# Value blending behind the chain, two tiles in turn, finer first transfers and new fillings in a hybrid decoder trunk

## The chip, the core and the metric

The kernel runs on one core of a Trainium2 chip. Its engines work side by side and meet only at semaphores: TensorE (PE) multiplies matrices, VectorE (DVE) and ScalarE (ACT) work elementwise, GpSimd (POOL) adds weights and issues transfers, SyncE (SP) issues transfers. SBUF is the memory that the engines read, PSUM the one that TensorE writes. The metric is the device time of one execution in microseconds; the table below gives it.

## The reference

One step of a trunk of two layers, for a prompt of 256 tokens and 8 sample tokens (264 columns) that share all weights. All is float32. Per layer:

```python
h = x @ w_in                                   # columns: mixer A, mixer B, merge gates
# mixer A, RWKV-7: token shift, decay, then a scan over time per head
S = S*w + (S @ a) b^T + v k^T ;  y = S @ r     # GroupNorm + bonus, times silu(z_A)
# in layer 1 the values are blended with those of layer 0 first:
vg = sigmoid(v0 + (v @ v1) @ v2) ;  v = v + (v_first - v) * vg
# mixer B, native sparse attention: compressed, selected and window branch,
# each softmax with a relative bias, gated per head, times silu(z_B)
m = sigmoid(g_A) * (o_A @ w_up_a) + sigmoid(g_B) * (o_B @ w_up_b)
x = layer_norm(ALPHA * x + m @ w_out)
```

The sample tokens read 256 earlier keys and values from pages of a cache and from a cache of window rows, and carry a 64x64 state per head.

## The kernel before

**Tiles of weights.** Activations lie transposed: `XT` holds 16 row tiles of 128 features by 264 columns, `H` the projected ones. A projected tile is 16 products of 128x128 weights (`WT`, two slots) with one tile of `XT`. One such product is a *unit*; the trace shows a unit as two instructions of line 760.

**Three kinds of product.** 46 tiles of a layer (`TILES`) are projected unit by unit by `project`. The others are computed in pairs of tiles with seven block products in place of eight (`main_pair`, `gate_pair`, `up_pair`, `out_pair`); those need sums of weight blocks, which POOL makes (`s1` the addition, `s3` the subtraction) and DVE (`s2`, `s4`), and sums of tokens, which DVE makes.

**The order, written by hand.** Each engine runs its own program. A layer goes: two tiles (`start`), 20 main pairs, four head quads of mixer A, the sample state, GroupNorm, compression, attention of the prompt (eight units), attention of the sample, four gate pairs, eight up pairs, eight out pairs, LayerNorm. From the head quads on these stages are chains of small products on PE with DVE and ACT between them. `plan()` gives each place in a chain a number of units (`BEHIND` for the quads, `BEHIND_MIX` after), and `project(place)` works tiles off up to that count while the chain's other engines compute. These are the *fillings*. What is left of the 46 tiles is worked off before the head quads' end (`mixers`) and before the gate pairs (`gates`). ACT takes each finished tile out of PSUM (`take_out`) at the same places.

**A head quad** (four heads, lines 1442 to 1501 on ACT, 1796 to 1917 on DVE, 979 to 1107 on PE): PE's `low` products; ACT's tanh; DVE computes decay, in layer 1 the blended values (`vd`, `vg`, `vm`, lines 1830 to 1834), then `kb`, `kf`, `kp`, `rk` (line 1843). PE fills with `low` units and waits for `rk` at line 1003. DVE goes on to `kt` (line 1856), for which PE waits at line 1012, then to the bonus (line 1859) and to `g4` (line 1865), which waits for line 1012.

**The sample's attention.** POOL loads the keys; when a product (`sc0`, `sc1`) has read them, it loads values into the same memory: per sequence two pages and one block of window rows (line 696). Line 1310 waits for them.

**Gate pair 0.** SP loads its four blocks when the attention's last DVE operation (`zb`, line 2145) is done, POOL then makes `s1` (line 715), which needs blocks 2 and 3, and `s3` (line 717), which needs 0 and 2.

**LayerNorm's tail** (lines 2323 to 2347): DVE centres the last four tiles, then tiles 0 to 11 in three operations (line 2328), waits for ACT's square root, takes the reciprocal (line 2339), multiplies in five groups (line 2343), scales tiles 12 to 15 (line 2346); ACT scales tiles 0 to 11 (line 1666). PE's first tile of layer 1 waits for these one by one.

**The first transfers.** SP loads `XT` in four parts and each tile of `WT` in two halves of 512 KB, in the order x, half, x, x, half, x, second tile, main pair 0.

Of the kernel before, what the change touches and what calls it, by code (L numbers as in the profile page):

```python
# [15 lines left out]
KT = D // P  # L16
# [72 lines left out]
HEAD_AT, HVAR_AT = 28, 48  # L89
FIRST = {}  # L90
# [25 lines left out]
def plan():  # L116

    upto = {}
    for L in range(DEPTH):
# [57 lines left out]
def hybrid_trunk(nc, ins, outs):  # L177
# [4 lines left out]
    with ExitStack() as ctx:  # L182
# [158 lines left out]
        d_x = [sem(f"x_loaded{q}") for q in range(4)]  # L341
        d_att = [sem("att_loaded0"), sem("att_loaded1")]
        st_shift, st_kv, st_wkv, st_swkv, st_win, st_y = (sem(n) for n in (
            "shift_stored", "kv_stored", "wkv_stored", "sample_wkv_stored", "window_copied", "y_stored"))
        w_in_slot = [[sem(f"weights_in_slot{s}{h}") for h in "ab"] for s in range(2)]
        w_in_main = [sem(f"weights_in_main{b}") for b in range(4)]
# [6 lines left out]
        def steps(phase, rounds, **engines):  # L353
            for e, names in engines.items():
# [9 lines left out]
              v=lambda it: ("lw one gate cum " + ("vd vg vm " if it >= NQUAD else "") + "kb kf kp rk at rt bt kt bon g40 g41 x0 x1 x2 lm1 "  # L364
# [23 lines left out]
        steps("os", DEPTH * BOTH, v="s2 s4", p="s1 s3")  # L388
        steps("ot", DEPTH, v="t1a t3a t2a t4a t1b t3b t2b t4b t1c t3c t2c t4c t1d t3d t2d t4d")
        steps("ln", DEPTH, t="head hvar mu var", v=" ".join(f"sum{i}" for i in range(1, HEAD)) + " hm hc0 sum12 sum13 hc1 hc2 ycb0 ycb1 d e" + "".join(f" yca{q}" for q in range(3)) + " rs "  # L390
              + " ".join(f"yn{q}" for q in range(5)) + " affv", a="hq0 hq1 hq2 hv sq0 sq1 sqrt " + " ".join(f"aff{i}" for i in range(SPLIT)))
# [72 lines left out]
        def _(sp):  # L464
            def load_x(q):
                sp.dma_start(XT[:, 4 * q:4 * q + 4, :], x_t[:, 4 * q:4 * q + 4, :]).then_inc(d_x[q], 16)
# [30 lines left out]
            def load_pairs(L):  # L497

                sp.wait_ge(*step("zb_v", L, "out"))
                for b in range(4):  # L500
                    load_block(L, 0, b)
# [42 lines left out]
            for n in range(DEPTH * N_TILES):  # L544
# [25 lines left out]
                for half in range(2):  # L570
                    sp.dma_start(WT[:, s, 8 * half:8 * half + 8, :], w_all[L, i, :, 8 * half:8 * half + 8, :]).then_inc(w_in_slot[s][half], 16)
                    if n == 0 and half == 0:
                        load_x(1)
                        load_x(2)
                    if n == 0 and half == 1:
                        load_x(3)
                    if n == 1 and half == 1:
                        for b in range(4):
                            load_main(L, 0, b)
            load_pairs(DEPTH - 1)  # L580
            for i, j in stores:
                if j <= SPLIT:
                    sp.wait_ge(*step("ln_a", DEPTH - 1, f"aff{j - 1}"))
                else:
                    sp.wait_ge(*step("ln_v", DEPTH - 1, "affv"))
# [4 lines left out]
        def _(po):  # L590
# [38 lines left out]
            for L in range(DEPTH):  # L629
# [69 lines left out]
                for g in range(BOTH):  # L699
# [3 lines left out]
                    if g:  # L703
                        po.wait_ge(*pair_step(L, g - 1, "st2"))
                        po.wait_ge(*step("os_v", L * BOTH + g - 1, "s2"))
# [20 lines left out]
        def _(pe):  # L726
# [6 lines left out]
            def project(*place):  # L733

                while at[0] < UPTO[place]:
# [4 lines left out]
                    if k == 0:  # L740
# [3 lines left out]
                        if L and i == s:  # L744
                            pe.wait_ge(*step("op_v", L * PAIRS - 1, "d3"))
                    if n == 0 and k % 4 == 0:
                        pe.wait_ge(d_x[k // 4], 16)
                    if k == 8:
                        pe.wait_ge(w_in_slot[s][1], 16 * loads_of_slot(L, i, u))
                    if kind == "lo" and L:  # L750
                        if k < SPLIT:
                            pe.wait_ge(*step("ln_a", L - 1, f"aff{k}"))
                        else:
                            pe.wait_ge(*step("ln_v", L - 1, "affv"))
# [1710 lines left out]
```

## Time and profile before

| | us |
|---|---|
| median of 3 runs (lowest, highest) | 2217.62 (2210.34, 2218.02) |
| the profiled execution | 2206.28 |
| its span, first to last instruction | 2204.6 |
| PE matmul busy | 2144.2 (97%) |
| DVE, ACT, POOL busy | 1067.2, 416.6, 509.5 |
| mean granted TensorE clock | 0.993 |

Busy time of PE is modelled at its ends and includes small stalls. A line of the trace names the engine, the source line of the kernel before, what is written and read, and in brackets how long the engine was idle before it and whom it waited for.

### The profile page before, as it was taken

Reading aid. Unit: us, or ns where it says so; the run is one execution under the profiler, and the core shown is the slowest. Engines: PE = TensorE matmul, PEld = TensorE weight load, DVE = VectorE, ACT = ScalarE, POOL = GpSimd, SP = SyncE. Lnnn points to the kernel's source line nnn. Section 1 sums busy time; section 2 is a strip of 40 time slices with the busy share of each in tenths; the row PEclk is TensorE's granted clock in tenths of the full one; section 3 lists DMA queues with packets and bytes.
Section 4 is the critical chain, followed back from the end, with each engine's and each line's share of the span. In section 5 each row is a group of like instructions: output and inputs, shape, how many; then the busy total and the mean of one; then the engine's idle time right before and its main releaser. Section 6 shows DMA issues by size and latency. Waiting matters only on the chain.

```text
span 2204.6 us, 48666 instructions
## 1 busy us (share of the span) xinstructions
PE 2144.2 (97%) x21460; PEld 1879.3 (85%) x21460; DVE 1067.2 (48%) x1753; ACT 416.6 (19%) x1169; POOL 509.5 (23%) x389
## 2 busy tenths in 40 slices
PE   8999999999999999999899999999999999999996
PEld 8999977777787679999799999777777876799996
DVE  3554344442835624774636443444428356247745
ACT  1111122222113511100211211122221135111002
POOL 3433300001111133433233341000011111233331
PEclk9999999999999999999999999999999999999998
DMA  8454332224642365555255443222246423655551
GB/s 295 166 171 164 116 135 99 99 98 182 226 154 77 104 230 171 167 179 172 92 180 172 162 165 133 90 94 86 95 173 225 154 77 103 223 173 172 169 174 62
DMA packets 87235, 329.50 MB, mean 149 GB/s; under 512 B 11824, under 2 KB 11840, under 8 KB 84720
## 3 DMA queue, kind: packets, MB, share of 16 engines
q1 hardware_dynamic: 73872, 268.60, 36.1%
q0 software_dynamic: 13152, 57.79, 7.4%
q8 instruction: 169, 2.77, 0.5%
q14 instruction: 42, 0.34, 0.0%
HBM read 315.91 MB, written 18.82 MB: 152 GB/s over the span
## 4 chain that ended last, share of the span: by engine, by line
PE 85%; DVE 7%; DMA 2%; ACT 2%; issue 2%; POOL 1%; POOLq 1%; SPq 0%; ACTq 0%; DVEq 0%
PE PB L760 22%; PE PB L776 3%; PE PB L803 3%; PE PB L799 3%; PE PB L794 3%; PE PB L789 3%; PE PB L785 3%; PE PB L779 3%; PE PB L1181 3%; PE PB L857 1%; PE PB L939 1%; PE PB L1012 1%; PE PB L922 1%; PE PB L924 1%; PE PB L917 1%
## 5 line engine op out<-in xcount | busy, mean ns | idle before, releaser
L760 PE MATMUL PB<-XT,WT 128*128 128x264 f32 (+1 forms) x2944 | 730.2, 397 | 11.8 <-DMA WT<-in_w_all 7.0
L760 PEld LDWEIGHTS PB<-XT,WT 128*128 128x128 f32 (+1 forms) x2944 | 533.9, 190 | 123.1 <-issue 23.9
L1371 ACT ACTIVATE VT<-PB 128x132 f32<-128x132 f32 (+2 forms) x256 | 69.7, 282 | 506.3 <-PE PB L789 130.6
L1371 ACT ACTIVATE ARENA<-PB 128x512 f32<-128x512 f32 (+5 forms) x197 | 88.4, 474 | 325.1 <-PE PB L1044 83.6
L592 POOL DMA_DIRECT2D out<-in_c_win x16 | 8.1, 506 | 514.0 <-DVE ARENA L1914 514.0
L592 POOL DMA_DIRECT2D ARENA<-in_c_sel x64 | 40.0, 625 | 239.1 <-issue 239.1
L613 POOL TENSOR_TENSOR TOEP<-WT 128x1024 f32<-128x1024 f32 x20 | 47.2, 2358 | 183.0 <-PE PB L789 183.0
L613 POOL TENSOR_TENSOR TOEP<-H 128x1024 f32<-128x1024 f32 x20 | 48.2, 2408 | 143.0 <-PE PB L789 143.0
L785 PE MATMUL PB<-ARENA,TOEP 128*128 128x132 f32 x640 | 78.6, 276 | 0.0
L789 PE MATMUL PB<-ARENA,TOEP 128*128 128x132 f32 x640 | 78.6, 276 | 0.0
L794 PE MATMUL PB<-ARENA,TOEP 128*128 128x132 f32 x640 | 78.6, 276 | 0.0
L803 PE MATMUL PB<-XT,TOEP 128*128 128x132 f32 x640 | 78.6, 276 | 0.0
L803 PEld LDWEIGHTS PB<-XT,TOEP 128*128 128x128 f32 x640 | 75.1, 190 | 0.0
L794 PEld LDWEIGHTS PB<-ARENA,TOEP 128*128 128x128 f32 x640 | 75.1, 190 | 0.0
L785 PEld LDWEIGHTS PB<-ARENA,TOEP 128*128 128x128 f32 x640 | 75.1, 190 | 0.0
L789 PEld LDWEIGHTS PB<-ARENA,TOEP 128*128 128x128 f32 x640 | 75.1, 190 | 0.0
L1181 PE MATMUL PB<-ARENA 128*128 128x288 f32 x256 | 62.7, 406 | 0.0
L1759 DVE TENSOR_TENSOR VT<-PB,VT 128x264 f32<-128x264 f32 x40 | 17.3, 433 | 93.4 <-PE PB L803 93.4
L1895 DVE TENSOR_TENSOR ARENA<-ARENA,PB 128x1024 f32<-128x1024 f32 x32 | 39.1, 1221 | 46.3 <-PE PB L1072 46.3
L1402 ACT ACTIVATE H<-PB 128x264 f32<-128x264 f32 x48 | 18.6, 388 | 223.4 <-PE PB L760 223.4
L1181 PEld LDWEIGHTS PB<-ARENA 128*128 128x128 f32 x256 | 48.6, 190 | 13.3
L2248 DVE TENSOR_TENSOR VT<-VT 128x132 f32<-128x132 f32 x32 | 47.7, 1529 | 24.1 <-ACT VT L1371 24.1
(435 smaller groups left out, 4154.9 us busy)
## 6 DMA issues: line engine op xcount, KB each, us to landing
WT<-in_w_all SPq DMA_DIRECT2D x344, 512.0 KB, 4.4
H<-in_w_all SPq DMA_DIRECT2D x120, 512.0 KB, 4.5
KNVC<-in_w_all SPq DMA_DIRECT2D x40, 512.0 KB, 3.7
out<-in_c_win POOLq DMA_DIRECT2D x16, 512.0 KB, 4.3
ARENA<-in_c_cmp POOLq DMA_DIRECT2D x64, 128.0 KB, 4.6
ARENA<-in_c_sel POOLq DMA_DIRECT2D x64, 128.0 KB, 3.1
ARENA<-in_c_win POOLq DMA_DIRECT2D x32, 256.0 KB, 3.8
TOEP<-in_toep POOLq DMA_DIRECT2D x2, 2048.0 KB, 8.0
```

The costliest lines, as they stand in the source:

```text
L592: po.dma_start(out, in_).then_inc(s, 16)
L613: mark("ms_p", it, add(OS1, w[2], w[3], ALU.add), "s1")
L760: ins = mm(PB[rows, bank, 0:T], WT[:, s, k, 0:rows.stop - rows.start], x, start=start, stop=stop)
L776: mm(a, w[0][:, k, :], XT[:, k, t0], start=k == 0, stop=k == BLK - 1)
L779: ins = mm(b, w[1][:, k, :], XT[:, BLK + k, t0], start=False, stop=k == BLK - 1, skip_group_check=True)
L785: mm(c, OS3[:, k, :], MT[:, 2, k, :], start=k == 0, stop=k == BLK - 1)
L789: ins = mm(d, OS1[:, k, :], MT[:, 0, k, :], start=False, stop=k == BLK - 1, skip_group_check=True)
L794: ins = mm(a, OS2[:, k, :], MT[:, 1, k, :], start=False, stop=k == BLK - 1, skip_group_check=True)
L799: ins = mm(c, w[3][:, k, :], MT[:, 3, k, :], start=False, stop=k == BLK - 1, skip_group_check=True)
L803: ins = mm(d, OS4[:, k, :], XT[:, BLK + k, t1], start=False, stop=k == BLK - 1, skip_group_check=True)
L1181: ins = mm(PB[:, 3 * (s // 8) + gp, 0:CMP_N], W1D[:, s, :], x, start=s % 8 == 0, stop=s % 8 == 7)
L1371: return act(out, in_, ACT.Copy)
```

## The change

Edits in the order of the kernel:

- *First transfers.* `XT` comes in five parts (2, 2, 4, 4 and 4 tiles), the first two weight tiles in quarters, both tiles' quarters in turn. Main pair 0's blocks come in the order 0, 2, 1, 3, and so do gate pair 0's.
- *Two tiles in turn.* The first two tiles of a layer are no longer worked off one after the other: for each k PE does one unit of each (`two_tiles`). In layer 1 DVE reports tiles 12 to 15 of the norm one by one.
- *Reciprocal moved up.* The third centring operation stands behind three of the multiplications.
- *Value blending moved.* `vd`, `vg`, `vm` stand behind `kt`, and ACT's copy of the sample's values waits for them, behind `take_out(low)`.
- *Window values.* ACT issues them, as soon as `sc0` and `sc1` are done; POOL issues pages alone.
- *Gate pair 0.* POOL makes `s3` first, then `s1`; PE waits for `s1` by itself.
- *Fillings.* `vec` 95 to 98, `mu` 4 to 5, `var` 9 to 10, `cb` 6 to 8, `cbt` 3 to 7; in layer 1 `low` of quads 1 to 3 has 18 in place of 16. `mixers` of layer 1 so falls from 11 to 5, `gates` of each layer from 37 to 26.

```diff
+X_PARTS = [0, 2, 4, 8, 12]
-BEHIND_MIX = {"v0": 4, "v1": 4, "v2": 4, "v3": 4, "vec": 95, "mu": 4, "mu2": 3, "sq": 0, "var": 9, "gbc": 5, "bc2": 5,
-BEHIND_MIX.update({"cb": 6, "cbt": 3})
+BEHIND_MIX = {"v0": 4, "v1": 4, "v2": 4, "v3": 4, "vec": 98, "mu": 5, "mu2": 3, "sq": 0, "var": 10, "gbc": 5, "bc2": 5,
+BEHIND_MIX.update({"cb": 8, "cbt": 7})
-    m = upto[L, hq, name] = min(m + n + (9 if hq == 0 and name == "low" else 0), first + FIRST["gb"] * KT)
+    m = upto[L, hq, name] = min(m + n + (0 if name != "low" else 9 if hq == 0 else 2 * L), first + FIRST["gb"] * KT)
...
             load_x(0)
-            for n in range(DEPTH * N_TILES):
+            load_quarter(0)
+            for q in range(1, len(X_PARTS)):
+                load_x(q)
+                if q > 1:
+                    load_quarter(q - 1)
+            for b in (0, 2, 1, 3):
+                load_main(0, 0, b)
+            for n in range(2, DEPTH * N_TILES):
...
-                        dma(SVS[odd][:, m, 2:4, :], c_win[L, b, :, 2:4, :], d_att[odd])
...
+                pair_loaded(po, L, 0, 0)
+                pair_loaded(po, L, 0, 2)
+                mark("os_p", L * BOTH, add(OS3, PW[0][0], PW[0][2], ALU.subtract), "s3")
+                pair_loaded(po, L, 0, 3)
+                mark("os_p", L * BOTH, add(OS1, PW[0][2], PW[0][3], ALU.add), "s1")
+                for g in range(1, BOTH):
...
+            def two_tiles(L):
+                for s in range(2):
+                    n = L * N_TILES + s
+                    if L:
+                        pe.wait_ge(w_in_slot[s][0], 16 * loads_of_slot(L, s, n // 2))
+                        pe.wait_ge(w_in_slot[s][1], 16 * loads_of_slot(L, s, n // 2))
+                        pe.wait_ge(tile_out[s], n // 2)
+                if L:
+                    pe.wait_ge(*step("op_v", L * PAIRS - 1, "d3"))
+                for k in range(KT):
+                    if L == 0 and k in X_PARTS:
+                        pe.wait_ge(d_x[X_PARTS.index(k)], 16)
+                    if L and k < SPLIT:
+                        pe.wait_ge(*step("ln_a", L - 1, f"aff{k}"))
+                    elif L:
+                        pe.wait_ge(*step("ln_v", L - 1, f"aff{k}"))
+                    for s in range(2):
+                        if L == 0 and k % 4 == 0:
+                            pe.wait_ge(w_first[s][k // 4], 16)
+                        ins = mm(PB[:, 6 + s, 0:T], WT[:, s, k, :], XT[:, k, :], start=k == 0, stop=k == KT - 1)
+                        if k == KT - 1:
+                            ins.then_inc(tile_done[s], 1)
+                at[0] += 2 * KT
...
 @@ ACT, head quad @@
-                    copy(vec(3), vs[:, :, SEQ:T])
                     copy(vec(4), KN[:, hp:hp + 2, SEQ:T])
-                    mark("rw_a", it, copy(vec(5), BB[:, :, SEQ:T]), "sv")
+                    copy(vec(5), BB[:, :, SEQ:T])
                     take_out(L, hq, "low")
+                    if L:
+                        wait(("rw_v", "vm"))
+                    mark("rw_a", it, copy(vec(3), vs[:, :, SEQ:T]), "sv")
...
+                def load_window_values(odd):
+                    sc.wait_ge(*step("as_t", L, f"sc{odd}"))
+                    for m in range(NB // 2):
+                        sc.dma_start(SVS[odd][:, m, 2:4, :], c_win[L, 2 * m + odd, :, 2:4, :]).then_inc(d_win[odd], 16)
+                load_window_values(0)
                 take_out(L, "as0")
+                load_window_values(1)
...
 @@ DVE, head quad: from behind wait("gate") to behind "kt" @@
+                    if L:
+                        v("vd", tt(TMP[:, :, :], VF[:, pair, :], H[:, hp + V0:hp + V0 + 2, :], ALU.subtract))
+                        wait("vd")
+                        v("vg", tt(TMP[:, :, :], TMP[:, :, :], AV[:, 1], ALU.mult))
+                        wait("vg")
+                        v("vm", tt(VS[:, :, :], H[:, hp + V0:hp + V0 + 2, :], TMP[:, :, :], ALU.add))
+                        wait("vm")
...
 @@ DVE, LayerNorm @@
-                for q in range(3):
+                for q in range(2):
                     centred(4 * q, 4, f"yca{q}")
...
+                    if q == 3:
+                        centred(8, 4, "yca2")
+                        own("ln_v", "yca2")
```

## Rows read from the trace of the kernel before

**Rows 1.** List of TensorE's waits: total us, times, longest us.
```profile
PE PB L1003 <- DVE ARENA L1843: 8.3, 3, 2.8
PE PB L760 <- DMA WT<-in_w_all: 7.0, 2, 6.7
PE PB L760 <- ACT XT L1666: 4.7, 1, 4.7
PE PB L1310 <- DMA ARENA<-in_c_win: 3.9, 2, 2.6
PE PB L1225 <- DVE ARENA L2073: 3.8, 2, 1.9
...
PE PB L731 <- DVE ARENA L1955: 2.3, 2, 1.2
...
PE PB L731 <- DVE ARENA L2060: 1.2, 2, 0.6
...
PE PB L1161 <- DVE ARENA L1967: 0.7, 2, 0.3
```

**Rows 2.** Timeline, head quad 1 of layer 1: start us, duration, engine, line, operation.
```profile
1435.99 7.28 PE L760 MATMUL PB<-XT,WT 128*128 128x264 f32 x32
1440.88 0.68 DVE L1830 TENSOR_TENSOR ARENA<-VF,H 128x528 f32<-128x528 f32 x1
1442.96 0.70 DVE L1835 TENSOR_TENSOR ARENA<-KNVC,ARENA 128x528 f32<-128x528 f32 x1
1446.05 1.16 PE L1003 MATMUL PB<-ARENA,CM 128*128 128x264 f32 x4 [2.78 <-DVE ARENA L1843]
1448.46 0.70 DVE L1859 TENSOR_TENSOR H<-PB,ARENA 128x528 f32<-128x528 f32 x1
1452.68 2.36 DVE L1865 TENSOR_TENSOR ARENA<-PB,CM 128x1024 f32<-128x1024 f32 x2 [3.52 <-PE PB L1012]
```

**Rows 3.** Stretches of 1 us; third from the end, the granted TensorE clock.
```profile
701.00:702.00 1.00, 1.00 (x5) 0.22 (x1) 0.93 (x4) 1.00 (x4) 0.00 (x0) 0.50 0.13 49
1094.00:1095.00 1.00, 1.00 (x3) 0.72 (x3) 0.96 (x4) 1.00 (x3) 0.00 (x0) 0.50 0.00 0
1581.00:1582.00 1.00, 1.00 (x4) 0.80 (x3) 1.00 (x4) 0.00 (x0) 0.00 (x0) 0.50 0.00 0
```

**Rows 4.** Timeline, LayerNorm of layer 0 and first tiles of layer 1.
```profile
1083.95 3.58 DVE L2328 SCALAR_TENSOR_TENSOR XT<-PB,XT 128x1056 f32<-128x1056 f32 x3
1085.88 0.48 ACT L1661 ACTIVATE ARENA<-PB,PD 128x264 f32<-128x264 f32 x1 [0.67 <-PE PB L1363]
1087.45 1.79 DVE L2339 RECIPROCAL ARENA<-ARENA 128x264 f32<-128x264 f32 x1
1090.49 17.26 PE L760 MATMUL PB<-XT,WT 128*128 128x264 f32 x64 [4.66 <-ACT XT L1666]
1090.64 5.59 ACT L1666 ACTIVATE XT<-XT,PT 128x264 f32<-128x264 f32 x11 [0.29 <-DVE XT L2343]
```

**Rows 5.** Chain that ended last, after the head quads of layer 1: start, us, what.
```profile
1643.45 8.46 DMA ARENA<-in_states
```

**Rows 6.** Timeline and a stretch of the start; last columns DMA share and GB/s.
```profile
6.74 16.82 PE L760 MATMUL PB<-XT,WT 128*128 128x264 f32 x64 [6.74 <-DMA WT<-in_w_all]
12.00:14.00 2.00, 1.86 (x9) 1.31 (x8) 0.07 (x1) 0.00 (x0) 0.00 (x0) 1.00 1.03 422
```

**Rows 7.** Timeline and a stretch, loading the sample's values in layer 0.
```profile
782.00:785.00 3.00, 3.00 (x16) 2.54 (x15) 1.55 (x6) 1.11 (x6) 1.77 (x4) 1.00 1.01 407
796.20 0.54 POOL L592 DMA_DIRECT2D ARENA<-in_c_win  x1
```

**Rows 8.** Timeline, from the sample's attention to gate pair 0, layer 0.
```profile
807.42 16.63 PE L760 MATMUL PB<-XT,WT 128*128 128x264 f32 x74
810.91 2.36 DVE L2145 SCALAR_TENSOR_TENSOR H<-H,ARENA 128x2112 f32<-128x2112 f32 x1
821.89 2.35 POOL L715 TENSOR_TENSOR TOEP<-KNVC 128x1024 f32<-128x1024 f32 x1 [25.16 <-DMA KNVC<-in_w_all]
```

More of the change, by code:

```diff
@@ L340, in hybrid_trunk @@
         d_pt, d_w2 = sem("page_table_loaded"), sem("cmp_out_loaded")
-        d_x = [sem(f"x_loaded{q}") for q in range(4)]
+        d_x = [sem(f"x_loaded{q}") for q in range(len(X_PARTS))]
         d_att = [sem("att_loaded0"), sem("att_loaded1")]
+        d_win = [sem("window_values0"), sem("window_values1")]
         st_shift, st_kv, st_wkv, st_swkv, st_win, st_y = (sem(n) for n in (
@@ L345, in hybrid_trunk @@
         w_in_slot = [[sem(f"weights_in_slot{s}{h}") for h in "ab"] for s in range(2)]
+        w_first = [[sem(f"first_weights{s}{q}") if q % 2 == 0 else w_in_slot[s][q // 2] for q in range(4)] for s in range(2)]
         w_in_main = [sem(f"weights_in_main{b}") for b in range(4)]
@@ L363, in hybrid_trunk @@
               a="th exp sv lt tok " + " ".join(f"y{j}" + (" tokb" if j == 1 else "") for j in lv) + " " + " ".join(f"r{c} u{c} o{c}" for c in ch),
-              v=lambda it: ("lw one gate cum " + ("vd vg vm " if it >= NQUAD else "") + "kb kf kp rk at rt bt kt bon g40 g41 x0 x1 x2 lm1 "
+              v=lambda it: ("lw one gate cum kb kf kp rk at rt bt kt " + ("vd vg vm " if it >= NQUAD else "") + "bon g40 g41 x0 x1 x2 lm1 "
                             + " ".join(f"lm{j + 1} z{j}" for j in range(1, LEVELS)) + f" z{LEVELS} st " + " ".join(f"d{c} s{c}" for c in ch)))
@@ L387, in hybrid_trunk @@
         steps("op", DEPTH * PAIRS, t="st1 st2 st3 st4p st4", v="a11 d1 a22 d2 a21 b22 d3")
-        steps("os", DEPTH * BOTH, v="s2 s4", p="s1 s3")
+        steps("os", DEPTH * BOTH, v="s2 s4", p=lambda it: "s1 s3" if it % BOTH else "s3 s1")
         steps("ot", DEPTH, v="t1a t3a t2a t4a t1b t3b t2b t4b t1c t3c t2c t4c t1d t3d t2d t4d")
-        steps("ln", DEPTH, t="head hvar mu var", v=" ".join(f"sum{i}" for i in range(1, HEAD)) + " hm hc0 sum12 sum13 hc1 hc2 ycb0 ycb1 d e" + "".join(f" yca{q}" for q in range(3)) + " rs "
-              + " ".join(f"yn{q}" for q in range(5)) + " affv", a="hq0 hq1 hq2 hv sq0 sq1 sqrt " + " ".join(f"aff{i}" for i in range(SPLIT)))
+        steps("ln", DEPTH, t="head hvar mu var", v=" ".join(f"sum{i}" for i in range(1, HEAD)) + " hm hc0 sum12 sum13 hc1 hc2 ycb0 ycb1 d e yca0 yca1 rs yn0 yn1 yn2 yca2 yn3 yn4 "
+              + " ".join(f"aff{i}" for i in range(SPLIT, KT)), a="hq0 hq1 hq2 hv sq0 sq1 sqrt " + " ".join(f"aff{i}" for i in range(SPLIT)))
         parts = [(0, 1), (1, 4), (4, 8), (8, 12), (12, 16)]
@@ L584, in _ @@
                 else:
-                    sp.wait_ge(*step("ln_v", DEPTH - 1, "affv"))
+                    sp.wait_ge(*step("ln_v", DEPTH - 1, f"aff{j - 1}"))
                 sp.dma_start(y_t[:, i:j, :], XT[:, i:j, :]).then_inc(st_y, 16)
@@ L826, in gate_pair @@
                     mm(c, OS3[:, k, :], OT[:, 2, k, :], start=k == 0, stop=k == BLK - 1)
+                if g == 0:
+                    pe.wait_ge(*step("os_p", sums, "s1"))
                 for k in range(BLK):
@@ L948, in _ @@
             for L in range(DEPTH):
-                project(L, "start")
+                two_tiles(L)
                 for m in range(MAINS):
@@ L1779, in _ @@
                     ve.wait_ge(*step("ln_a", L - 1, f"aff{SPLIT - 1}"))
-                    ve.wait_ge(*step("ln_v", L - 1, "affv"))
+                    ve.wait_ge(*step("ln_v", L - 1, f"aff{KT - 1}"))
                 else:
-                    for q in range(4):
+                    for q in range(len(X_PARTS)):
                         ve.wait_ge(d_x[q], 16)
```

46 lines of the change are left out of this document (13 added, 33 removed).

## The prediction, made before the changed kernel was run

> **What bounds the kernel now.** First the list of TensorE's waits [rows 1]. The profiled execution is 2206.28 us (span 2204.6, 1.68 around it). TensorE (PE) is nearly always at work, so a change can only take away a wait, an early stretch before the first matmul, the tail after the last, or time at the low clock. Each line of rows 1 gives total, times and longest: 8.3 us are three waits for line 1843 in the head quads of layer 1, 3.9 are two for the window values, 3.8 are two behind the second score product, 2.3 the end of the sample state, 4.7 the first matmul of layer 1, 7.0 the kernel's start.
>
> Then the granted clock in windows of 1 us [rows 3], with one window for each kind of fall. It is at the lower of its two levels (1.2 of 2.4 GHz) from 700.4 to 703.4 and again from 1802.9 to 1806.3, where PE had waited 0.6 and 1.9 us shortly before; from 1580.9 to 1584.3, after the third head-quad wait; from 1089.3 to 1096.1, after 3.5 us of rest; and at the end. Half speed over 3.4 us of work costs 1.7 us.
>
> Last the timelines of these places. A projection unit (one k of one tile, the filling) is two instructions; 32 of them take 7.28 us, 0.455 us a unit [rows 2]. Filling that moves into a wait shortens the rest of the layer by its length; moved where PE does not wait, it changes nothing.
>
> **Head quads of layer 1.** The blending is three VectorE (DVE) operations, 1440.88 to 1442.96, 2.08 us, ahead of line 1843. PE ends its 16 units at 1443.27 and waits 2.78 us until 1446.05 [rows 2]. After, line 1843 ends near 1443.95 and the filling of 18 units at 1444.18: no wait. The later quads repeat it, so 8.3 us go (2.08 of each by the move, 0.7 by filling), and with the third wait its fall of the clock, 1.7. The blending comes back behind line 1856. DVE's work up to line 1859 is the same, so that still ends at 1449.16, while PE's product before it (start 1448.92, end 1452.68 by the wait of line 1865) now ends near 1450.5: 1.3 us of cover. ScalarE's (ACT) copy that now waits for the blending, about 1448.9, fits in it too, and `low`'s take-out moves ahead of that wait. Quad 0 of layer 1 shows no wait and gains nothing.
>
> The six units (3 quads x 2) come out of the stretch between the last quad and the sample state's end, where the states' load sets the time [rows 5]. `vec` gets 3 back, so 3 x 0.455 = 1.4 us of new wait there: 1.2 becomes 2.6. Sum: 8.3 + 1.7 - 1.4 = **8.6**. If a clock fall comes with that wait, 1.7 less; rests of 2.6 to 2.8 us passed without one three times and fell once (rows 1 and 3), so I count none.
>
> **Fillings.** Layer 0: three units cover the 1.2 of `vec` [rows 1], **1.2**. `mu` and `var` cover line 1967's 0.7, **0.7**. `cb` covers 0.6 twice, **1.2**. The four units of `cbt` stand ahead of score product 1, and the wait of 1.9 is for the addition that needs that product: it moves along and stays. But PE works longer before it, which may hold the clock: between 0 and 1.5 + 1.7; no row decides, I take half, **1.6**. The 11 units a layer leave the last filling, 37 to 26, 5.0 us shorter. What then must be in time is gate pair 0. Line 2145 ends at 813.27, the filling began at 807.42, and POOL's first sum, which waits for all the blocks, starts at 821.89 [rows 8]. With 26 units gate pair 0 begins at 807.42 + 11.83 = 819.25; it needs the subtraction (s3) two products of 1.8 us later, 822.85, and the addition (s1) at 824.65. In the new order of loads s3 can start when two blocks are in, about 818.5, and ends at 820.9; s1 starts at 821.9 and ends at 824.25. Cover 0.4 us: **0** lost, up to 5 a layer if the loads come late (below). POOL and SP queue nothing else there; the next block load still waits for the DVE sum behind s1, so nothing is overwritten early.
>
> **Window values.** POOL issues 24 transfers for the sample values, a third of them these, the last at 796.20; PE waits for it, 1.3 and 2.6 us [rows 1, 7]. Without the eight, POOL is done some 8 x 0.54 = 4.3 us sooner. ACT issues eight a layer; no row shows an ACT issue, so 0 to POOL's 0.54 each, 2.2 for four at most ahead of the softmax, and 36 units (16 us) cover that chain. 0 to 3.9 can go; **3.5**. In 782 to 785 the DMA engines are full (1.01, 407 GB/s) [rows 7], which speaks for less. The Trainium skill (DMA: Bandwidth & Descriptors, "Issuing engines are not separate DMA queues") says that issuing from several engines saves only issue time, all running on the same engines; by it alone this term could be 0. The issue time saved exceeds both waits, so I keep most of it.
>
> **Start.** PE's first matmul is at 6.74, when 528 + 512 KB have come, and 64 instructions take 16.82 us where 64 x 0.2275 = 14.56 would do [rows 6]. Now 264 + 256 KB suffice for the first and 256 more for the second: near 5.0. Two tiles a step use about 1 MB in 3.64 us, 285 GB/s, and the queue gives 422 once it runs [rows 6], so PE is hardly starved; its slow first part (2.3 us lost) stays. End of the tiles near 21.5 instead of 23.56: **2.0**, between 0 and 2.8. Main pair 1's loads now wait for both tiles, 21.5 instead of 16.5, and must be in when POOL sums them, near 29: covered. If transfers half the size ran at half the rate, 211 GB/s, the 4.6 MB (tokens 2.1, two tiles 2.1, parameters 0.4) would take 22 us and the tiles would end near 24: 0.4 lost. The Trainium skill (the same page, "Measured") advises 1 MiB or more a transfer and lists 138 GB/s at 64 KB against 341 at 1 MB; by it the start would be no gain. The row of 782 to 785 is against it: 407 GB/s with pieces of 128, 256 and 512 KB in flight.
>
> **Layer boundary and end.** The square root is ready at 1086.36, but the reciprocal waits for the third centring, 3.58 / 3 = 1.19 us, and begins at 1087.53 [rows 4]. After, it begins at 1086.4: PE starts 1.15 us sooner. The two tiles cost 17.26 us for 14.56 of work, 2.7 at the low clock. The rest of PE is then 3.5 us, as long as before the fall in this trace, so I keep the fall; PE starts as it comes, and loses 1.7 to 2.7, I say 2.1: 0.6 gained. At full clock a tile in turn would be held by ACT's 0.51 us a step (5.59 / 11) against 0.455; two tiles take 0.91 and are not, but at half clock they were not held before either: 0 for that edit. **1.75**, between 0.5 and 3.9. The kernel's end repeats the pattern: ACT starts 1.15 sooner and gives part back waiting for the moved centring; 0 to 1.15, **0.7**.
>
> **Sum.** 8.6 + 1.2 + 0.7 + 1.2 + 1.6 + 3.5 + 2.0 + 1.75 + 0.7 = 21.25 us: 2206.28 becomes 2185.0. The median of the runs is 2217.62, 11.3 above the profiled execution; the same subtraction gives 2196.
>
> **Rivals.**
> *Gate pair 0 comes late.* Pair 1's loads now stand directly behind pair 0's; if they share the engines, its last block lands up to 5 us later (2 MB at 422 GB/s), s1 ends at 829, PE waits 4.6 us and loses 2.7 to the clock as at the layer boundary: 7.3 a layer, 14.6. For: 8.6 us between line 2145 and s1, long for 2 MB. Against: at the start one queue's transfers landed in order. 2196 + 14.6 = 2211.
> *The head quads' wait moves* to the blended values, behind the first product of line 1012: 2.08 x 3 comes back and the fall: 2196 + 7.9 = 2204. Against: 1.3 us of cover.
> *Small first transfers are slow:* 2.4 back, 2198.5.
> *The clock holds* at the boundary and in both attention stages: 2.1 + 1.6 more, 2192.
> *Slower:* the clock falls in a head quad and does not come back, because that stage's matmuls are small; it decides from the first fall that lasts a whole quad. A quad has 74 units, 33.7 us at full clock, as much again at half: 2196 + 33.7 = 2230. For: one fall did come there. Against: it ended after 3.4 us.
>
> **How the numbers follow.** Forecast 61%, its own range 2188 to 2204; late gate pair 14%, moved wait 9%, slow transfers 4%, clock holds 8%, slower 4%. The range 2184 to 2211 leaves out the slower case and the tails. 0.5% (11 us) is about what a measurement of this kernel can tell from no change. Faster by more: nearly all of the forecast, the clock case, most of the moved wait and slow transfers, a tenth of the late pair, 78%. Within: most of the late pair and the rest, 17%. Slower 5%.
>
> **What would show it.** Line 1843's wait gone from the list and no new one at the product behind line 1859; the wait on line 1955 near 0 in layer 0, near 2.6 in layer 1; no wait for window values; the two-tile line starting near 5.0 and the second one 3.5 us after the norm's last matmul; gate pair 0 without a wait. Wrong if a wait of some us stands at the third or fourth product of gate pair 0 (lines 826 and 828 before), or if the low clock covers a long stretch.

## The result: 2195.7 us, 0.9912 of before, and the profile after

The changed kernel takes 2195.73 us (median of 5 runs, 2191.28 to 2200.17) against 2214.74 of before (5 runs on the same chip): ratio 0.9912, 95% interval 0.9889 to 0.9936. Run a second time it took 2194.39 against 2213.75, ratio 0.9916 (0.9892 to 0.994). The forecast was 2196. The profiled executions, 2191.28 and 2206.28, lie only 15.0 apart, the medians 19.0.

TensorE's list of waits after, as [rows 1] (total us, times, longest us):

```profile
PE PB L786 <- DMA WT<-in_w_all: 7.0, 2, 5.3
PE PB L1253 <- DVE ARENA L2112: 3.8, 2, 1.9
PE PB L786 <- ACT XT L1704: 3.6, 1, 3.6
PE PB L761 <- DMA WT<-in_w_all: 3.3, 5, 1.7
...
PE PB L861 <- DVE VT L2258: 1.8, 2, 0.9
...
PE PB L741 <- DVE ARENA L1994: 1.6, 1, 1.6
PE PB L741 <- DVE ARENA L2137: 1.5, 1, 1.5
...
PE PB L811 <- POOL TOEP L623: 0.3, 1, 0.3
```

The 8.3 us of the head quads and the 3.9 of the window values are gone, and 4.7 at the boundary between the layers became 3.6. The start is 7.0 as before, in two pieces. New are fillings that wait for weights (3.3), gate pair 0 (1.8), 1.5 behind the second score product, and a short wait at main pair 1 (0.3). Of the 3.3, 0.41 and 0.67 stand in the sample's attention, and the longest one stands in the filling `vec` of layer 1, just ahead of the group norm (start us, duration, engine, line, operation):

```profile
1646.15 36.76 PE L761 MATMUL PB<-XT,WT 128*128 128x264 f32 x164 [1.73 <-DMA WT<-in_w_all]
```

The same by stage, from the start of each stage's first product in the two traces (minus: shorter than before):

| stretch | change, us |
|---|---|
| start to end of the first two tiles | +0.30 |
| main pairs of layer 0 | +0.54 |
| head quads to group norm, layer 0 / 1 | 0.00 / -7.96 |
| group norm to gate pair 0, layer 0 / 1 | -1.76 / -4.91 |
| gate pairs, layer 0 / 1 | +1.49 / +1.06 |
| LayerNorm and first two tiles of layer 1 | -2.14 |
| LayerNorm at the end | -1.62 |

(The end of the first two tiles is taken as the start of the next product, here and below: 23.40 before, 23.70 after. In each layer three units more, 1.4 us, now lie ahead of the group norm and not behind it, so the gains ahead of it are really 1.4 and 9.3, and behind it 0.4 and 3.5. The sum is -15.0.)

Head quad 1 of layer 1 after (start us, duration, engine, line, operation), as [rows 2]:

```profile
1434.10 8.17 PE L761 MATMUL PB<-XT,WT 128*128 128x264 f32 x36
1442.11 1.10 PE L1031 MATMUL PB<-ARENA,CM 128*128 128x264 f32 x4
1444.46 0.70 DVE L1890 TENSOR_TENSOR ARENA<-VF,H 128x528 f32<-128x528 f32 x1
1445.94 0.71 DVE L1894 TENSOR_TENSOR ARENA<-H,ARENA 128x528 f32<-128x528 f32 x1
1446.68 0.71 DVE L1898 TENSOR_TENSOR H<-PB,ARENA 128x528 f32<-128x528 f32 x1
1448.68 2.35 DVE L1904 TENSOR_TENSOR ARENA<-PB,CM 128x1024 f32<-128x1024 f32 x2 [1.29 <-PE PB L1040]
```

36 instructions (18 units) and then the product without a wait; the blending runs behind, beside TensorE's next work, and L1904 now waits 1.29 us where it waited 3.52: the 1.3 us of cover of the prediction are there.

### The profile page after: what moved, and what is told of

Its sections match the earlier page's. It is cut to its first block, busy times and chain, and to the rows that moved or that the text cites. A ratio compares the mean times of both kernels' runs of the same rounds, so it can differ in the third digit from the quotient of the medians.

```text
span 2189.6 us, 48679 instructions
## 1 busy us (share of the span) xinstructions
PE 2141.2 (98%) x21460; PEld 1877.5 (86%) x21460; DVE 1071.1 (49%) x1753; ACT 416.6 (19%) x1169; POOL 501.8 (23%) x373
## 3 DMA queue, kind: packets, MB, share of 16 engines
q8 instruction: 169, 2.77, 0.5%
## 4 chain that ended last, share of the span: by engine, by line
PE 90%; DVE 5%; DMA 4%; issue 0%; POOL 0%; ACT 0%; SPq 0%; DVEq 0%; POOLq 0%; ACTq 0%
PE PB L761 25%; PE PB L811 3%; PE PB L829 3%; PE PB L825 3%; PE PB L820 3%; PE PB L815 3%; PE PB L802 3%; PE PB L805 3%; PE PB L1209 3%; DMA WT<-in_w_all 2%; PE PB L786 1%; PE PB L885 1%; PE PB L967 1%; PE PB L1040 1%; PE PB L950 1%; PE PB L952 1%
## 5 line engine op out<-in xcount | busy, mean ns | idle before, releaser
L761 PE MATMUL PB<-XT,WT 128*128 128x264 f32 (+1 forms) x2816 | 696.7, 395 | 3.5 <-DMA WT<-in_w_all 3.3
L761 PEld LDWEIGHTS PB<-XT,WT 128*128 128x128 f32 (+1 forms) x2816 | 505.7, 189 | 110.4 <-issue 19.2
L1602 ACT ACTIVATE ARENA<-ARENA 128x128 f32<-128x128 f32 (+1 forms) x128 | 56.2, 443 | 16.2 <-DVE ARENA L2115 16.2
```

The costliest lines, as they stand in the source:

```text
L761: ins = mm(PB[rows, bank, 0:T], WT[:, s, k, 0:rows.stop - rows.start], x, start=start, stop=stop)
L1602: ins = act(x, x, ACT.Exp, bias=NM[u % 3][:, t, i:i + 1], accum_out=RSM[u % 3][:, t, i:i + 1])
```

## The experiments

Each is the changed kernel with one edit or, in two, several of them. Where no ratio is given, the reading is from one profiled execution.

### 1. Blending in front again

```
-                    if L: v("vd" ...); v("vg" ...); v("vm" ...)     # behind "kt"
+                    if L: v("vd" ...); v("vg" ...); v("vm" ...)     # behind wait("gate")
```

> The changed kernel with one part undone: the three blending operations stand in front of VectorE's chain again; the filling of 18 units in the head quads of layer 1 stays. Theory A (the move is worth 2.08 us a quad, the two more units 0.91): the wait at the product behind `low` comes back three times with 2.78 - 0.91 = 1.87 us, 5.6 in all, and the stage from the first head quad of layer 1 to the group norm grows by 5.6, by up to 1.7 more if a fall of the clock comes with it. Rival B (the filling alone had done it, because TensorE waits for something else beside the blending): the three waits are under 0.3 us and the stage stays within 1 us. Rival C (the blending behind the chain costs something there that now goes): the stage grows by less than 4.

Measured: 2203.53 us, ratio to before 0.9962 (0.9948 to 0.9976). TensorE's timeline at the three places (in brackets the wait and whom it was for):

```profile
1447.25 1.05 PE L1031 MATMUL PB<-ARENA,CM 128*128 128x264 f32 x3 [1.88 <-DVE ARENA L1881]
1515.76 1.73 PE L1031 MATMUL PB<-ARENA,CM 128*128 128x264 f32 x4 [1.89 <-DVE ARENA L1881]
1583.67 0.68 PE L761 MATMUL PB<-XT,WT 128*128 128x264 f32 x2 [2.33 <-ACT H L1422]
```

and the windows behind them (third number from the end: granted clock):

```profile
1449.00:1450.00 1.00, 1.00 (x4) 0.80 (x3) 1.00 (x3) 0.00 (x0) 0.00 (x0) 0.50 0.00 0
1517.00:1518.00 1.00, 1.00 (x4) 0.79 (x3) 1.00 (x3) 0.00 (x0) 0.00 (x0) 0.50 0.00 0
1585.00:1586.00 1.00, 1.00 (x4) 0.80 (x3) 1.00 (x2) 0.00 (x0) 0.00 (x0) 0.50 0.72 283
```

Theory A: 1.88 and 1.89 us, 1.87 expected; the third shows at the filling in front, 2.33. But the clock fell behind all three, for 3.4 us each, so the stage grew by 11.45 (6.1 of waits, 5.1 of half speed), not by 5.6 to 7.3. The move is the largest part of the change, and in this profile nearly half of it comes by way of the clock (before the change, one fall stood behind the three waits). None of the twelve other profiles of kernels with the blending moved shows a fall in these quads.

### 2. Parameters issued later

```
+            po.wait_ge(w_first[1][0], 16)
             dma(PT[:, :, :], par, d_par)
```

> The changed kernel, with the two parameter transfers and the page table on GpSimd's queue issued only when the second tile's first weight quarter has landed. In the changed kernel TensorE starts at 5.32, waits 1.69 us from 6.5 to 8.22 for that quarter, and ends the two tiles at 23.70. Theory A (the 0.4 MB of parameters share the DMA engines with the first quarters): the quarter lands near 6.5, the second wait is under 0.4 us, the tiles end between 22.0 and 22.5. Rival B (DMA is slow in its first microseconds whatever is in flight, so 264 + 512 KB take until 8.2): the quarter lands within 0.3 us of 8.2 and the tiles end near 23.7. Rival C (TensorE's slow first instructions set the end): the wait goes, but the tiles end within 0.4 us of 23.7.

Measured: start at 5.14, no second wait, tiles end at 22.16. That looked like theory A, but it did not hold: the same edit within experiment 6 started at 5.13, waited 1.11 and ended at 23.79, and the changed kernel itself, run again, started at 5.15, waited 0.27 and ended at 21.74. One profile could not decide this. What differs from one execution to the next is when the second tile's first quarter lands, 4.5 to 6.5 us after its issue; why, stays open.

### 3. Products ahead of the first tiles

```
+            pe.wait_ge(d_warm, 1)                    # VectorE has set VF[:, 0, :] to 1.0
+            for _ in range(10):
+                mm(PB[:, 0, 0:T], VF[:, 0, 0:P], VF[:, 0, :], start=True, stop=True)
```

> The changed kernel with ten products on a constant ahead of the first two tiles, into a bank that is not used yet (they add nothing to the result). In seven looks at kernels with this start the two tiles ended between 21.7 and 25.2: each time the first instructions after a rest went at half pace (0.81 us each against 0.39; 3 to 4 begin in a microsecond against 6) for some 3 to 6 us, and where TensorE rested for the second quarter, this began anew. Theory A (the end of the tiles is set by the slow pace after rest): with the products from 1 to about 7 us the tiles run at 6 instructions a microsecond from the first on and end between 21.0 and 22.8, even if they start as late as 8. Rival B (the pace is that of the transfers, whose rate is 160 to 210 GB/s from 4 to 5 us): the tiles still begin with 3 to 4 instructions a microsecond and end at 23 or later.

TensorE's timeline of the start in the changed kernel:

```profile
5.32 1.22 PE L786 MATMUL PB<-XT,WT 128*128 128x264 f32 x2 [5.32 <-DMA WT<-in_w_all]
8.22 15.64 PE L786 MATMUL PB<-XT,WT 128*128 128x264 f32 x62 [1.69 <-DMA WT<-in_w_all]
```

and two of its windows (behind the length: TensorE's busy time and instructions):

```profile
9.00:10.00 1.00, 1.00 (x4) 0.79 (x3) 0.00 (x0) 0.70 (x1) 0.00 (x0) 1.00 1.05 407
10.00:11.00 1.00, 1.00 (x3) 0.72 (x3) 0.00 (x0) 0.00 (x0) 0.00 (x0) 1.00 1.04 419
```

The same of the experiment, timeline and windows:

```profile
1.33 7.22 PE L742 MATMUL PB<-VF 128*128 128x264 f32 x20 [1.33 <-DVE VF L1807]
8.39 14.40 PE L790 MATMUL PB<-XT,WT 128*128 128x264 f32 x64
```

```profile
9.00:10.00 1.00, 1.00 (x6) 0.84 (x6) 0.17 (x4) 0.99 (x1) 0.00 (x0) 1.00 1.07 419
10.00:11.00 1.00, 1.00 (x6) 0.87 (x5) 0.00 (x0) 0.29 (x1) 0.00 (x0) 1.00 1.04 419
```

Theory A. At much the same DMA rate (407 and 419 GB/s against 419 and 419) the tiles go at 6 instructions a microsecond from the first on, 64 in 14.40 us, and end at 22.63, though they start at 8.39. In the changed kernel the first two instructions at 5.32 gain nothing: TensorE rests again, and from 8.22 the slow pace lasts another 3.2 us, until 11.45.

The slow pace is that of the clock's lower level, although the column says 1.00. The trace's record of the clock begins only at 11.45 us in the changed kernel and at 6.43 in the experiment, and in each of the fourteen traces it begins where the step from one instruction of the first products to the next falls from 0.44 to 0.22 us; the 1.00 of the windows ahead of it stands for no record. At the boundary of the layers, where the record says 0.50, the step is 0.44 too: the window of 1094 to 1095 in [rows 3] has the same two numbers for TensorE and its weight loads, 1.00 (x3) and 0.72 (x3), as the one of 10 to 11 above.

### 4. Gate pair 0: one addition first

```
+                ve.wait_ge(*step("gp_a", L * GATES, "c"))
+                mark("gp_v", ..., tt(FM[0][:, 0:HALF], ..., PB[:, 2, HALF:T], ALU.add), "f11")
                 second_sum(0)
                 fourth_sum(0)
```

> The changed kernel with one VectorE addition of gate pair 0 (the one into FM that the fifth group of products waits for) ahead of the pair's second and fourth sums instead of behind them. Theory A (VectorE's order holds TensorE there: its inputs are there from 827.0 on, but it comes third, at 831.12): the waits of 0.93 and 0.83 us before that product go to under 0.15, and each layer from the gates to the up pairs is 0.7 to 0.9 us shorter. Rival B (the second sum, which comes from GpSimd's late first sum, holds it too): 0.3 to 0.6 of the wait stays, named for the sum. Rival C: the wait comes back at the last product of the pair, for the fourth sum, and nothing is gained.

Timeline of the changed kernel there:

```profile
826.15 2.35 POOL L709 TENSOR_TENSOR TOEP<-KNVC 128x1024 f32<-128x1024 f32 x1 [0.74 <-DMA KNVC<-in_w_all]
828.61 1.22 DVE L2200 TENSOR_TENSOR TOEP<-TOEP,H 128x1024 f32<-128x1024 f32 x1 [6.58 <-POOL TOEP L709]
829.87 1.22 DVE L2212 TENSOR_TENSOR TOEP<-H,TOEP 128x1024 f32<-128x1024 f32 x1
831.12 0.29 DVE L2258 TENSOR_TENSOR VT<-VT,PB 128x132 f32<-128x132 f32 x1
831.56 1.70 PE L861 MATMUL PB<-ARENA,TOEP 128*128 128x132 f32 x13 [0.93 <-DVE VT L2258]
```

and of the experiment:

```profile
822.33 2.36 POOL L709 TENSOR_TENSOR TOEP<-KNVC 128x1024 f32<-128x1024 f32 x1 [0.50 <-DMA KNVC<-in_w_all]
823.54 0.29 DVE L2224 TENSOR_TENSOR VT<-VT,PB 128x132 f32<-128x132 f32 x1 [5.04 <-ACT VT L1400]
824.79 1.23 DVE L2200 TENSOR_TENSOR TOEP<-TOEP,H 128x1024 f32<-128x1024 f32 x1 [0.96 <-POOL TOEP L709]
826.64 1.96 PE L861 MATMUL PB<-ARENA,TOEP 128*128 128x132 f32 x16
```

Theory A. VectorE idles 6.58 us for GpSimd's sum while an addition whose inputs are ready stands behind it; put first, it costs nothing. Both waits go; the stage is +0.11 and 0.00 against before, instead of +1.49 and +1.06, which is more than the 0.7 to 0.9 expected. Here GpSimd's sum also came a little sooner, 2.9 us after the pair's first product against 3.2; where it comes later, as in experiment 6, TensorE waits for it all the same.

### 5. Fillings of the prompt's attention moved

```
-BEHIND_MIX.update({"cb": 8, "cbt": 7})                        "as1": 36
+BEHIND_MIX.update({"cb": 8, "cbt": 3, "sc1": 4})   # sc2: 1 -> 4    "as1": 33
                 scores(1)
+                project(L, "sc1")
```

> The changed kernel with other fillings in the prompt's attention of both layers: the one ahead of score product 1 (cbt) 7 to 3 units, 4 units between score products 1 and 2, behind score product 2 4 instead of 1, and 33 instead of 36 in the sample's attention, so that the sum is unchanged. Theory A (the wait of 1.92 us at score product 2 stands there because no filling lies between products 1 and 2; the 1.49 behind it likewise): both waits go in both layers, the stretch from the score products to the gates is 3.4 us shorter in layer 1, 1.9 to 3.9 in layer 0. Rival B (ScalarE's exponentials, 5.6 us a unit, set the pace): the waits come back at the next unit's products and under 1 us is gained. Rival C: the three units less before the sample's values bring the wait for them back, 1.4 us at most a layer.

Measured: the wait at score product 2 is gone in both layers; of the one behind it 0.16 us is left, and 0.23 and 0.40 us for ScalarE a little later. From the score products to the gates, layer 1 is 3.6 us shorter than the changed kernel (-8.64 against before, where that was -5.01). Layer 0 is 2.1 us shorter from the group norm to the gates than in the changed kernel, with 6.8 us of low clock in either profile (one fall of 6.8 here, two of 3.4 there). No wait for the sample's values came back.

### 6. Three together, and the changed kernel again

Experiments 2, 4 and 5 in one kernel.

> The changed kernel with the parameters' transfers behind the second tile's first quarter, VectorE's addition of gate pair 0 first, and the fillings of the prompt's attention moved, all three together. If the three effects add up: tiles end near 22.2 (1.5 less), no wait before the fifth products of gate pair 0 (0.9 less a layer), no waits at score product 2 and behind it (3.4 less in layer 1, 1.9 to 3.4 in layer 0): 8.6 to 10 us less than the changed kernel in the same call, near 2187 on the median. Rival (the time freed in the attention is given back, since gate pair 0 then begins earlier against its loads, or the clock falls there more often): 4 us or less gained, with a wait at gate pair 0's third or fourth products or low-clock stretches of 5 us and more in both attention stages.

> The changed kernel itself, unaltered, beside the others on the same chip. Expected 2195.7 us, ratio to before 0.991. In its profile the places with a fixed cause repeat within 0.2 us (the boundary of the layers 2.1 below before, the wait of 0.8 to 0.95 at gate pair 0, 1.9 at score product 2), while the low clock in the two attention stages, and the wait behind score product 2 with it, differ from the first profile by up to 5 us. If instead the low clock there belongs to the new fillings, the same falls come again at the same places: in layer 0 only, 3.5 and 3.3 us long.

Measured: 2186.27 us, ratio to before 0.9870 (0.9847 to 0.9894), and 2194.39 for the changed kernel beside it: 8.1 less, a little under the 8.6 to 10 expected. Beside experiment 11, whose interval overlaps, this is the fastest version. The waits of the prompt's attention are gone as in experiment 5; the start, 23.79, gave nothing; and at gate pair 0 of layer 0 a wait for GpSimd's sum `s1` has come in place of the one for VectorE:

```profile
825.04 2.07 PE L857 MATMUL PB<-ARENA,TOEP 128*128 128x132 f32 x16 [0.68 <-POOL TOEP L710]
```

That stage is +1.04 against before in layer 0 and 0.00 in layer 1. The rival, that gate pair 0 now begins too early against its loads, came true in this one place.

In the changed kernel's second profile the waits of fixed cause repeat (3.61 at the boundary, 0.94 and 0.93 at gate pair 0, 1.92 at score product 2 twice). The falls of the clock repeat in part: in layer 0 both come again, 1.2 and 14.8 us behind the first score product as in the first profile, the second of them 6.8 us long in place of 3.4; one in layer 1 is new; and at the boundary the fall lasts 6.8 us in place of 3.4, so that the boundary gained 0.89 and not 2.1. Windows of the first profile, then of the second:

```profile
691.00:692.00 1.00, 1.00 (x3) 0.22 (x2) 0.88 (x3) 0.05 (x1) 1.00 (x2) 0.50 0.57 209
1782.00:1783.00 1.00, 1.00 (x5) 0.40 (x4) 0.97 (x4) 0.00 (x0) 0.56 (x2) 1.00 0.66 180
```

```profile
691.00:692.00 1.00, 1.00 (x4) 0.82 (x3) 0.90 (x4) 0.00 (x0) 0.82 (x2) 0.62 0.78 258
1782.00:1783.00 1.00, 1.00 (x5) 0.46 (x2) 0.88 (x3) 0.05 (x1) 0.92 (x2) 0.50 0.75 291
```

Over the thirteen profiles of the changed kernel and its variants, the prompt's attention of layer 0 has one or two falls of 3 to 7 us in ten, that of layer 1 in six. The two profiles with the old fillings, the kernel before and experiment 8, have falls in both layers. So the new fillings neither bring the falls about nor do away with them; whether they make them rarer, two profiles can't tell.

### 7. Window values back on GpSimd

```
-                    sc.dma_start(SVS[odd][:, m, 2:4, :], c_win[...]).then_inc(d_win[odd], 16)
+                        dma(SVS[odd][:, m, 2:4, :], c_win[...], d_win[odd])     # in GpSimd's loop
```

> The changed kernel with the eight transfers of window values a layer back on GpSimd's queue, between its page transfers. Theory A (GpSimd's issuing, not the DMA engines, made them late): the wait for them comes back with 1.0 to 1.6 us in layer 0 and 2.3 to 2.9 in layer 1, 3.9 in all. Rival B (the values share the engines with the next weights, so the changed kernel only pays elsewhere): the waits of fillings for weights in the sample's attention, 0.41 in layer 0 and 0.67 in layer 1, go at the same time, and the net is 2.5 to 3. Rival C (other edits took the wait away): no wait comes back.

Measured: rival C, no wait for the values. GpSimd's last issue comes 25.4 to 25.8 us after the stage's first product in both layers, before and here, but it lands sooner here. The last value's transfer of layer 1 (KB, us to landing), before and then here:

```profile
ARENA<-in_c_win POOLq DMA_DIRECT2D x1, 256.0 KB, 7.9
```

```profile
ARENA<-in_c_win POOLq DMA_DIRECT2D x1, 256.0 KB, 4.4
```

Before, a weight tile's two transfers of 512 KB were issued within 1.7 us ahead of it; here they come within 2 us behind it. The new fillings move TensorE by some units against its tiles, and the tiles' loads with them. That the nearby loads are what delays the value is read from these issue times; no run moved them alone.

### 8. The old fillings

```
+"vec": 95, "mu": 4, "var": 9, "cb": 6, "cbt": 3      (98, 5, 10, 8, 7)
```

> The changed kernel with the five fillings of before (vec 95, mu 4, var 9, cb 6, cbt 3), everything else as changed; the window values stay on ScalarE's queue. With them on GpSimd's queue, but the new fillings, no wait for them was left, so either the fillings or the queue alone may have done it. Theory A (as predicted: GpSimd done 4 us sooner is enough by itself): no wait for sample values in either layer. Theory B (the wait belongs to the phase of the loads: the last values came while a weight tile's 1 MB was in flight, 6.2 and 7.9 us to landing against 4.0 and 4.4, and the fillings shift the weight loads): a wait of 0.5 to 2.6 us for the values is back in one layer or both. Beside it: the waits of 1.2 (vec), 0.3 and 0.6 come back in layer 0, and gate pair 0, which begins 5 us later against its loads, has no wait for VectorE or GpSimd, so that each layer gains 0.9 to 1.5 there and gives 2 to 3 elsewhere.

Measured: theory A, no wait for the values either. So, by one profile of each, either of the two edits alone takes that wait away. With ScalarE as issuer a filling waits 0.57 us for its weights (0.41 and 0.67 in the changed kernel, none in experiment 7): part of the delay seems to have gone from the values to the weights. At gate pair 0 no wait is left (+0.09 and 0.00). In front of the group norm the waits are 1.30 and 3.33 (in the changed kernel 0 and 1.60, in its second profile 0.66 and 0.52), and 0.33 each behind it.

### 9. Reciprocal behind all centrings again; 10. first tiles of layer 1 one after the other

```
-hc1 hc2 ycb0 ycb1 d e yca0 yca1 rs yn0 yn1 yn2 yca2 yn3 yn4
+hc1 hc2 ycb0 ycb1 d e yca0 yca1 yca2 rs yn0 yn1 yn2 yn3 yn4
```

> The changed kernel with the reciprocal of the LayerNorm behind all three centrings again. Theory A (the reciprocal waited for the third centring): the wait of the two-tile line of layer 1 is 4.6 to 4.8 instead of 3.61, the boundary and the end of the kernel are each 1.0 to 1.2 us longer, and the boundary's low-clock stretch is as long as now, 3 to 3.7 us, unless its length comes from the wait; if it does, it is 6 to 7 us as before the change, and the boundary grows by 2.1. Rival B (the two tiles in turn, not the reciprocal, brought the 2.1 us at the boundary): it grows by less than 0.5, the end by less than 0.5.

```
-                two_tiles(L)
+                project(L, "start") if L else two_tiles(L)
```

> The changed kernel with the first two tiles of layer 1 one after the other again, the reciprocal as changed. With the reciprocal put back, the boundary of the layers was still 1.1 us shorter than before at the same wait of 4.66 us; either the two tiles in turn give that, or the length of the low-clock stretch there, which was between 3.5 and 7.5 us in nine looks. Theory A (as predicted, the tiles in turn give nothing): the same wait of 3.61 us, 64 instructions in 14.6 us and half the low-clock time on top, and the boundary is 0.9 to 2.3 below before, by that stretch alone. Rival B (one tile in turn is held by ScalarE's 0.51 us a step at full clock): further waits for ScalarE or VectorE of 0.3 us and more in all between the first tile's instructions, and the 64 take longer than 14.6 plus half the low-clock time.

The 64 instructions of the boundary in the two experiments:

```profile
1092.98 16.16 PE L786 MATMUL PB<-XT,WT 128*128 128x264 f32 x64 [4.66 <-ACT XT L1704]
```

```profile
1090.11 16.40 PE L768 MATMUL PB<-XT,WT 128*128 128x264 f32 x64 [3.61 <-ACT XT L1714]
```

The reciprocal is worth 1.05 us at the boundary (4.66 against 3.61) and 0.91 at the end (19.65 against 18.74 us from the mean's product to the end). The two tiles in turn are worth at most 0.2: without them the boundary is 1.91 shorter than before, with them 2.14; 16.40 is within 0.15 of 14.56 and half of 3.4 us at the low clock, and no further wait stands in it. What is left of the 2.14 is the length of the fall: 6.8 us before; 3.4 in ten of the thirteen profiles since, 6.8 in two, and in experiment 11 one of each.

The end of the kernel gained 1.62, so 0.7 of it is not the reciprocal's. With the reciprocal put back, the last store is still issued 0.31 us sooner than before and lands in 3.27 us instead of 3.68; no run shows why.

### 11. A last version

Experiments 3, 4 and 5 together.

> The changed kernel with the ten products ahead of the first tiles, VectorE's addition of gate pair 0 first, and the fillings of the prompt's attention moved (parameters issued as in the changed kernel). If the parts add up by their single looks: about 1 us at the start (tiles end near 22.6 instead of 23.6 on average), 1.8 at the two gate pairs, 3.4 in layer 1 and 1.9 to 3.4 in layer 0: 8 to 10 us less than the changed kernel, 2185 to 2187 on the median, ratio to before near 0.987. Rival (the scatter of the low clock in both attention stages hides it): 4 us or less, ratio 0.989 or more.

Measured: 2186.44 us, ratio 0.9885 (0.9869 to 0.9902): by the median what was expected, but no better than experiment 6. The tiles end at 23.04, 0.75 sooner than in experiment 6. The intervals, some 7 to 10 us wide, can't show that; and in this profile two falls make the boundary 0.80 longer than before, and the gate pairs of layer 1 are +0.71, behind GpSimd's sum.

## Why the prediction was right in the sum, and where its steps failed

**Head quads (8.6).** Right: the waits, the 1.3 us of cover, and the place where the six units are missed. In the profiled pair the stage gives 9.3 with the three moved units counted. The rival of a wait that moves to the blended values did not come (no wait at the next product). At the group norm of layer 1 the forecast had one wait of 2.6; there are two, 1.73 for weights in `vec` and 1.60 for line 1994 (1955 before). The clock fall behind them, which the prediction counted as none, is absent in this pair, but four of the twelve profiles with the blending moved have one there, behind waits of 1.98 to 3.33; the other eight, with waits of 0.52 to 2.77, have none.

**Fillings (4.7).** `vec` in layer 0 and `mu`, `var`, `cb` in both layers took their waits away as forecast (in the second profile 0.66 is left behind `vec`). The step that failed is "PE works longer before it, which may hold the clock", 1.6: falls come in ten of thirteen profiles in layer 0, and in both with the old fillings. Where the clock is high at that place, a wait of 1.5 behind the second product appears that the low clock had hidden. The prediction saw that the wait of 1.9 moves along with `cbt`, and left it there; a filling behind score product 1 takes it (experiment 5).

**Gate pair 0 (0).** Failed, at the step "Cover 0.4 us: 0 lost". s1 ended 5.55 us after the pair began, where 5.0 was worked out (it waited 0.74 for its blocks): the cover was used up, and TensorE's fourth product began 0.21 late. The larger part was overlooked: VectorE's own order, in which the addition `f11` (line 2258) stands behind the two sums that wait for s1. 1.5 and 1.1 us were lost. Reordering recovered both in experiment 4, and in experiments 6 and 11 one layer of two; in the other the blocks came later, as the rival of the late gate pair says, but at 0.5 to 0.7 us of wait and not 4.6.

**Window values (3.5).** The waits went, 3.9 of them, and 1.1 came back as fillings that wait for weights. The step "the issue time saved exceeds both waits" holds by itself: GpSimd's last issue came 3.8 and 4.3 us sooner in its stage, where 4.3 was worked out, and with the old fillings the move alone took both waits away (experiment 8). It was not needed, though, which the prediction missed: with the new fillings the old issue order has no wait either (experiment 7). The Trainium skill (DMA: Bandwidth & Descriptors, "Issuing engines are not separate DMA queues") says that all issuers share the same engines; experiment 7 agrees, 7.9 against 4.4 us for the same transfer from the same queue, with SyncE's weight loads ahead of it and behind it. What the prediction drew from it, that by it alone the term could be 0, is not borne out (experiment 8).

**Start (2.0).** Failed, at two steps. "Near 5.0" was to have the first quarter of both tiles in: the first matmul came at 5.32, but the second tile's quarter landed at 8.2, and TensorE rested again. And "PE is hardly starved; its slow first part stays": the slow part does not stay as long as it was, it is paid again after the second rest. The tiles ended at 23.70 (21.5 forecast), and between 21.7 and 25.2 in nine profiles with this start. The rival of slow small transfers has the end nearly right (near 24) but not the cause: the rate is not halved, it reaches 407 GB/s. Up to 7 us 1.24 MB had come against 1.44 before (the sum of the windows of 1 us), less by a seventh.

"Covered", of main pair 1's loads behind the two tiles, failed as well. GpSimd waited for them until 35.62, where its sums had begun at 30.86 before, and TensorE for GpSimd; the main pairs grew by 0.54, and in the profile whose tiles ended last, at 25.17, by 1.53:

```profile
35.62 2.35 POOL L620 TENSOR_TENSOR TOEP<-WT 128x1024 f32<-128x1024 f32 x1 [9.25 <-DMA WT<-in_w_all]
```

**Boundary and end (2.45).** Right for the reciprocal (1.05 and 0.91 measured, 1.15 and up to 1.15 forecast), right that two tiles in turn give next to nothing. "I keep the fall" failed: it lasted 3.4 us and not 6.8, which gave the other 1.1 of the boundary. The 0.7 at the very end that the reciprocal does not explain was in no term.

**The sum.** 21.25 was forecast on the profiled execution, 15.0 came, 6.3 too few. That 2196 was met on the median is luck, with two parts. First, the medians lie 19.0 apart and not 15.0. The profiled execution of before had a mean granted clock of 0.993, its eleven runs beside experiment 6 had 0.987 to 0.992, the changed kernel's runs beside them 0.991 to 0.994. A thousandth is some 4.4 us at half speed, 2.2 us of time; so, as an estimate from these clocks, the 4 us more are falls that before mostly has and its profile had not. Experiment 1, with a fall behind each of its three waits, suggests where; the runs that were not profiled can't show it. Second, the forecast started from a median of 2217.62, which two more runs brought down to 2214.74, 2.9 lower. 6.3 too few in the terms and 4.0 and 2.9 from elsewhere cancelled.

## What to carry to other kernels

A wait is paid twice where the clock falls behind it, as in experiment 1; count the falls over several executions, not in the one that was profiled. When an operand is given earlier, look at the order on the engine that consumes it: an addition that is ready must not stand behind one that waits. And start an engine once: here the work that was brought forward into a stretch that ended in another rest gained nothing. Last, a wait for a transfer may depend on what other transfers are issued beside it, which any shift of the schedule moves.

## What the runs showed of the hardware

TensorE begins the program at the pace of the lower clock level, 0.44 us from one instruction of the first products to the next against 0.22, although the clock column of those windows says 1.00: the trace has no record of the clock there, and the record begins where the pace doubles, 6.4 to 14.3 us into the program. In the nine profiles with a second rest of more than 1 us the pace doubled 3.0 to 6.0 us after that rest, 6.1 to 8.8 after the first instruction; in the five without one, 4.0 to 5.9 after the first instruction. The length of a rest alone did not decide a fall of the clock: 2.78 us passed without one twice before the change, 1.88 and 1.89 us brought one each (experiment 1). And in all starts the DMA rate dips: with the finer pieces to 122 to 208 GB/s from 4 to 5 us, before to 232 from 5 to 6; then it rises to 400 and more. What causes the dip was not found, and it was there without the parameter loads as well (206 and 208).
